# A two-layer encoder kernel on one core: early sums at the stage beginnings, and the latents' norm taken in the RWKV projections

## The chip, the cores and the metric

The kernel runs on one core of a Trainium2 chip. Its engines are TensorE (PE: matmuls; PEld: its weight loads), VectorE (DVE), ScalarE (ACT), GpSimd (POOL) and SyncE (SP), which issues all transfers here. They run side by side and meet at semaphores. The metric is the device time of one launch in microseconds; lower is better.

## What is computed

Sixteen meta tokens and 512 tokens, 1024 channels wide, pass through two layers. Cut to what matters here:

```
h = concat(meta, x)                                   # 528 x 1024
for l in range(2):
    h = h + 0.5 * rms(swiglu(rms(h, g0)), g1)
    u = rms(h, g2)
    p_rw, p_ml, p_dsa, p_gate = split(u @ w_in[l])
    y_rw, y_ml, y_dsa = rwkv7(p_rw), mlstm(p_ml), dsa(p_dsa)
    proj = branches @ w_branch[l]
    mixed = sum(sigmoid(p_gate) * proj) @ w_out[l]
    h = h + rms(mixed, g3)
    h = h + 0.5 * rms(swiglu(rms(h, g4)), g5)
# in dsa: q, c_kv, q_idx, k_idx, w_idx = split(p)
#   c_kv = rms(c_kv, kv_norm);  q_lat[h] = (q[h] @ w_uk[h]) / 8        # 8 heads of 64, latent 128
#   an index score picks 128 of the allowed positions; attention of q_lat on c_kv;
#   y = (prob @ c_kv) @ w_uv
```

## The kernel before, in words

Activations lie channels by tokens: `h` is eight tiles of 128 channels by 528 tokens, and 528 tokens are two PSUM banks of 264. The kernel is a row of stages, each a block of per-engine programs closed by a barrier: start; then in each layer FFN, RWKV (projections, recurrence, output), DSA, mLSTM, merge, FFN; at the end a post-norm and the store.

**Exact products.** A float32 product is three products of a faster type: each operand is split into a high part (ScalarE copy) and a low part (a subtraction, on GpSimd for weights in FFN, RWKV and merge, on VectorE in DSA). `exact` issues high times high, high times low, low times high. Weights come as units of four 128x128 blocks, 256 KB, through a ring; `S("split")` or `S("d_split")` counts units whose low part is made. Float32 matmuls that are not split run as two passes each, and the profile counts passes.

**A stage beginning (class `Lead`, from L315).** The stage before leaves its output in `fo` and the squares of its output channels in `ssq`: seven of eight tiles summed in `ssq[:, 2]` by `Out.add`, the last in `ssq[:, 1]`. `tensor_post` sums both over the channels on TensorE (L367; a matmul with the squares as weights and 64 columns of ones for each of five token groups), VectorE and ScalarE make the root (L409 to L412, L335), and TensorE spreads it over the channels (L374). Then for each k of eight VectorE multiplies `fo` (L429), adds to `h` (L430), and makes `u_low` (L424) from ScalarE's `u_high` (L347); ScalarE also makes the squares of `h` (L350), which TensorE sums (L400). TensorE multiplies k's block for two output tiles at once (`leading_pair`, or the loop in `phase_ffn`), 12 matmuls, as soon as `u_low` is there. The factor of this second norm is applied to the outputs. `occupy` is 128x128 matmuls on ones whose result nobody reads (L384; L831 in merge); seven such stand at the end of FFN and merge, after `out_put` has reached 5, four and twelve in a beginning.

ScalarE's order in a beginning: root, then the first two weight splits (L634, L1631), then `u_high` and squares by k, with the third split behind k=0 and the fourth behind k=1.

**RWKV projections.** 14 tiles of RWKV columns, then ten of DSA's go through one `Dense` ring of four units. GpSimd sets `s3` (L969) before its first low part. VectorE scales each tile by the row factor (L996).

**DSA beginning (`phase_dsa`, from L1695).** SyncE loads `wuk` and `wuv`, then the dense weights. ScalarE squares the latents `ckv` (L1904), TensorE sums them over channels (L1813), VectorE takes mean and reciprocal (L1973, L1974), ScalarE the root, VectorE scales (L1976). TensorE waits for all three loads, then makes `q_lat` of eight heads (L1822, 64 rows each) in two PSUM pairs in turn, ScalarE copies them out (L1910), then come eight blocks of dense work, the values (L1830), which VectorE copies out (L1984), and the first index products (L1764). ScalarE makes three weight splits behind the fourth head.

Of the kernel before, what the change touches and what calls it, by code (L numbers as in the profile page):

```python
# [13 lines left out]
ds = bass.ds  # L14
# [37 lines left out]
EARLY = 4  # L52

# [46 lines left out]
def build_program(nc, x, meta_tokens, norm_gain, ffn_w_in, ffn_w_out, w_in, rw_mu, rw_w0, rw_w_up,  # L100
# [4 lines left out]
    with ctx:  # L105
# [53 lines left out]

        def clear():  # L160
# [24 lines left out]
        def token_spread(lhs, m):  # L185
# [3 lines left out]
            return last  # L189

# [48 lines left out]
        def phase_start(st):  # L239
            xt = sb(st, "xt", [P, 5, D_MODEL])  # L240
            firstp = Params(st)
            with nc.Block() as block:
# [8 lines left out]
                def _(g):  # L251
# [5 lines left out]
                    g.memset(ones[:], 1.0)  # L257
# [30 lines left out]
                def _(pe):  # L288
# [12 lines left out]
                    firstp.turn(pe, PS[:, 2])  # L301

# [12 lines left out]
        class Lead:  # L315
# [6 lines left out]
            def __init__(self, st, ring, pre, banks, later):  # L322
# [3 lines left out]
                self.sums = PS[:, banks[0]]  # L326
# [37 lines left out]
            def column_sums(self, src, first, last):  # L364

                for j, (t0, n) in enumerate(ST_):
                    ins = nc.tensor.matmul(self.sums[0:n, 64 * j:64 * j + 64], src[:, t0:t0 + n], ones[:, 0:64],  # L367
                                           start=first and j == 0, stop=last, skip_group_check=True)
                return ins

# [22 lines left out]
            def tensor_square(self, pe, k):  # L393
                pe.wait_ge(S("squares"), k + 1)
                if not self.later:
                    self.column_sums(self.ring[k % 2], k == 0, k == KD - 1).then_inc(S("h_summed"), 1)
                    self.occupy(pe, 1 if k < KD - 1 else 4)
                    return
# [5 lines left out]
            def factor(self, v, own, x):  # L404
# [4 lines left out]
                nc.vector.tensor_scalar(rq[:, 0:full], self.sums[:, 0:64 * full:64], 1.0 / D_MODEL, EPS, ALU.mult, ALU.add)  # L409
                own(nc.vector.tensor_scalar(rq[0:m, full:full + 1], self.sums[0:m, 64 * full:64 * full + 1], 1.0 / D_MODEL,  # L410
# [3 lines left out]
            def vector(self, v):  # L414
# [101 lines left out]
        def phase_ffn(hh, hl, l, which, pre, gain, cut):  # L516

            with ExitStack() as st:
# [15 lines left out]
                with nc.Block() as block:  # L534
# [36 lines left out]
                    def _(pe):  # L571
# [18 lines left out]
                        for k in range(KD):  # L590
                            pe.wait_ge(S("u_low"), k + 1)
                            for s in range(2):
                                n = 2 * (k // 4) + s
                                if k % 4 == 0:
                                    pe.wait_ge(S("split"), n + 1 + R)
                                product(s, n, k % 4, k)
# [27 lines left out]
                        else:  # L624
                            pe.wait_ge(S("out_put"), KD - 3)
# [1917 lines left out]
```

## Time and profile before

| | |
|---|---|
| median of 3 runs | 3551.43 us (3547.36 to 3555.32) |
| profiled execution | 3546.51 us, span 3544.8 us |
| mean granted TensorE clock | 0.978 |
| TensorE busy | 3390.9 us, 96% of the span |
| VectorE, ScalarE, GpSimd busy | 1554.5, 1185.2, 1260.0 us |
| stages of layer 0 start at | FFN 15.7, RWKV 422.7, its recurrence 614.0, its output 802.7, DSA 827.4, mLSTM 1071.2, merge 1181.7, FFN 1372.4 us |
| of layer 1 | 1777.7, 2183.4, 2376.2, 2566.0, 2592.3, 2836.0, 2945.7, 3128.9 us; post-norm 3517.6 |

An operation's row gives start, duration, engine, line, what it writes and reads, the number of like operations in a row, and in brackets how long its engine had idled and what ended that. The granted clock is a share of full speed; 1.00 is 2.4 GHz and 0.50 is 1.2 GHz. A row of a stretch gives its bounds, its length, the busy time and number of instructions of PE, PEld, DVE, ACT and POOL, the granted clock, the DMA engines' busy share and GB/s.

### The profile page before, as it was taken

How to read it: one execution, taken by the hardware profiler on the slowest of the kernel's cores; microseconds unless marked ns; L12 is line 12 of the kernel's file. 1: busy time of each engine (PE TensorE's matmuls, PEld its weight loads, DVE VectorE, ACT ScalarE, POOL GpSimd, SP SyncE). 2: the span in 40 equal slices, each digit the busy share in tenths (PEclk: the TensorE clock that was granted, in tenths of full speed). 3: DMA queues.
4: the chain of work that ended last, by engine and by line, in shares of the span. 5: the costliest groups of instructions: out<-in, count | busy, mean ns of one | idle time of the engine just before them, and what ended most of it. 6: DMA issues, size and time to landing. Idle time of an engine off the chain costs nothing. (4 is left out here: it accounts for less than half of the span.)

```text
span 3544.8 us, 74221 instructions
## 1 busy us (share of the span) xinstructions
PE 3390.9 (96%) x30010; PEld 3068.4 (87%) x30010; DVE 1554.5 (44%) x2696; ACT 1185.2 (33%) x2257; POOL 1260.0 (36%) x936
## 2 busy tenths in 40 slices
PE   8999999998999999999999999999989999999998
PEld 8999999776778899999999999987767777878886
DVE  5331245445767434332053313454457684343312
ACT  3222342222455324222232223412235453342222
POOL 4444335320003443444434443343200024535542
PEclk9999999998999999999999999999989999999999
DMA  3333222001112232333223332210011122323332
GB/s 97 89 91 90 81 63 57 3 3 45 48 34 60 64 92 67 93 91 90 77 84 89 91 91 77 66 45 3 3 51 46 31 60 75 95 72 95 95 91 73
DMA packets 464410, 236.55 MB, mean 67 GB/s; under 512 B 20862, under 2 KB 462476, under 8 KB 464156
## 3 DMA queue, kind: packets, MB, share of 16 engines
q1 hardware_dynamic: 464156, 232.92, 23.5%
q8 instruction: 189, 3.10, 0.4%
q14 instruction: 65, 0.53, 0.0%
HBM read 230.50 MB, written 2.10 MB: 66 GB/s over the span
## 5 line engine op out<-in xcount | busy, mean ns | idle before, releaser
L561 POOL TENSOR_TENSOR W_low<-W,W_high 128x512 fp32r<-128x512 f32 (+1 forms) x544 | 720.8, 1326 | 877.7 <-ACT W_high L634 876.9
L156 PE MATMUL PS<-u_high,W_high 128*128 128x264 f32 (+1 forms) x2944 | 903.9, 307 | 15.6 <-DVE u_low L424 7.2
L157 PE MATMUL PS<-u_low,W_high 128*128 128x264 f32 (+1 forms) x2944 | 891.8, 303 | 0.0
L158 PE MATMUL PS<-u_high,W_low 128*128 128x264 f32 (+1 forms) x2944 | 891.6, 303 | 0.0
L634 ACT ACTIVATE W_high<-W 128x512 fp32r<-128x512 f32 (+1 forms) x544 | 335.5, 619 | 991.6 <-PE PS L158 954.7
L156 PEld LDWEIGHTS PS<-u_high,W_high 128*128 128x128 f32 x2944 | 554.5, 188 | 47.6 <-DVE u_low L424 9.6
L157 PEld LDWEIGHTS PS<-u_low,W_high 128*128 128x128 f32 x2944 | 555.0, 189 | 22.7
L158 PEld LDWEIGHTS PS<-u_high,W_low 128*128 128x128 f32 x2944 | 552.9, 188 | 22.5
L156 PE MATMUL PS<-u_high,dW_high 128*128 128x264 f32 (+1 forms) x1408 | 429.7, 305 | 15.6 <-POOL dW_low L1636 4.6
L158 PE MATMUL PS<-u_high,dW_low 128*128 128x264 f32 (+1 forms) x1408 | 405.0, 288 | 0.0
L157 PE MATMUL PS<-u_low,dW_high 128*128 128x264 f32 (+1 forms) x1408 | 404.8, 287 | 0.0
L157 PE MATMUL PS<-hidden_low,W_high 128*128 128x264 f32 (+1 forms) x1232 | 369.9, 300 | 0.0
L158 PE MATMUL PS<-hidden_high,W_low 128*128 128x264 f32 (+1 forms) x1232 | 368.9, 299 | 0.0
L156 PE MATMUL PS<-hidden_high,W_high 128*128 128x264 f32 (+1 forms) x1232 | 368.3, 299 | 0.0
L156 PEld LDWEIGHTS PS<-u_high,dW_high 128*128 128x128 f32 (+1 forms) x1408 | 270.1, 192 | 34.3 <-issue 15.6
L157 PEld LDWEIGHTS PS<-u_low,dW_high 128*128 128x128 f32 (+1 forms) x1408 | 270.4, 192 | 2.3
L158 PEld LDWEIGHTS PS<-u_high,dW_low 128*128 128x128 f32 (+1 forms) x1408 | 269.0, 191 | 0.0
L679 DVE TENSOR_TENSOR hid<-PS,rs 128x528 f32<-128x528 f32 (+1 forms) x88 | 61.9, 703 | 405.7 <-PE PS L158 404.5
L756 POOL TENSOR_TENSOR W_low<-W,W_high 128x512 fp32r<-128x512 f32 x120 | 168.6, 1405 | 197.9 <-ACT W_high L764 197.9
L156 PEld LDWEIGHTS PS<-hidden_high,W_high 128*128 128x128 f32 x1232 | 232.1, 188 | 7.4
L158 PEld LDWEIGHTS PS<-hidden_high,W_low 128*128 128x128 f32 x1232 | 231.8, 188 | 7.6
L157 PEld LDWEIGHTS PS<-hidden_low,W_high 128*128 128x128 f32 x1232 | 231.2, 188 | 7.9
(383 smaller groups left out, 5485.3 us busy)
## 6 DMA issues: line engine op xcount, KB each, us to landing
W<-in_ffn_w_in SPq DMA_DIRECT2D x352, 256.0 KB, 2.9
dW<-in_w_in SPq DMA_DIRECT2D x172, 256.0 KB, 2.9
W<-in_ffn_w_out SPq DMA_DIRECT2D x160, 256.0 KB, 2.8
W<-in_w_in SPq DMA_DIRECT2D x80, 256.0 KB, 3.0
W<-in_w_branch SPq DMA_DIRECT2D x48, 256.0 KB, 2.9
W<-in_w_out SPq DMA_DIRECT2D x32, 256.0 KB, 2.9
W<-in_ffn_w_out SPq DMA_DIRECT2D x32, 128.0 KB, 2.1
xt<-in_x SPq DMA_DIRECT2D x4, 512.0 KB, 4.6
```

The costliest lines, as they stand in the source:

```text
L156: nc.tensor.matmul(dst, wh, xh, start=first, stop=False)
L157: nc.tensor.matmul(dst, wh, xl, start=False, stop=False)
L158: return nc.tensor.matmul(dst, wl, xh, start=False, stop=final)
L561: g.tensor_tensor(WL[:, r, 0:nk], W[:, r, 0:nk], WH[:, r, 0:nk].bitcast(F32), ALU.subtract).then_inc(S("split"), 1)
L634: nc.scalar.activation(WH[:, r, 0:nk], W[:, r, 0:nk], ACT.Copy).then_inc(S("high"), 1)
L679: nc.vector.tensor_tensor(cut.of(hid[:, j]), ps(1), cut.of(rs[:]), ALU.mult).then_inc(dve_evac, 1)
L756: g.tensor_tensor(WL[:, u % R], W[:, u % R], WH[:, u % R].bitcast(F32), ALU.subtract).then_inc(S("split"), 1)
```

## The change

What it does:
1. The sums over `ssq[:, 2]` move to the end of the stage before (`early_sums`, into bank 4), with five fillers behind them instead of seven; in the start stage they run on zeros.
2. The first two output tiles take the two products with `u_high` for each k first, then the one with `u_low`. VectorE makes `u_low` of k-1 before it adds k. In FFN all of the first four weight splits stand ahead of `u_high` on ScalarE. In RWKV the setting of `s3` moves behind the eighth low part.
3. The latents' square, sum, root and scaling move into the RWKV projections, around block 168 of 192. `wuk` takes the buffer of `lora` and loads in RWKV's output part.
4. In DSA the heads start at once, in three PSUM pairs, each followed by three 128x128 fillers. Two weight splits are made during the heads, one behind the fourth and one behind the sixth, the others behind the eight dense blocks. SyncE issues two dense units ahead of `wuv`.

```diff
+        def token_square_sums(bank, src, first, last):
+            for j, (t0, n) in enumerate(ST_):
+                ins = nc.tensor.matmul(PS[0:n, bank, 64 * j:64 * j + 64], src[:, t0:t0 + n], ones[:, 0:64],
+                                       start=first and j == 0, stop=last, skip_group_check=True)
+            return ins
+        def early_sums(pe):
+            pe.wait_ge(S("out_put"), KD - 1)
+            pe.wait_ge(S("added"), KD - 2)
+            token_square_sums(POST_BANK, ssq[:, 2], True, False)
...
             def tensor_post(self, pe):
-                self.column_sums(ssq[:, 2], True, False)
-                self.column_sums(ssq[:, 1], False, True).then_inc(S("summed"), 1)
+                token_square_sums(POST_BANK, ssq[:, 1], False, True).then_inc(S("summed"), 1)
                 self.occupy(pe, 4)
...
                 for k in range(KD):
                     own(nc.vector.tensor_tensor(fo[:, k], fo[:, k], self.spread, ALU.mult))
-                    nc.vector.tensor_tensor(h[:, k], h[:, k], fo[:, k], ALU.add).then_inc(S("h_new"), 1)
                     if self.later and k:
                         low(k - 1)
+                    nc.vector.tensor_tensor(h[:, k], h[:, k], fo[:, k], ALU.add).then_inc(S("h_new"), 1)
...
                         for k in range(KD):
+                            pe.wait_ge(S("u_high"), k + 1)
+                            j, tiles = k % 4, [(s, a, cut.span(a)) for s in range(2) for a in range(cut.a)]
+                            for s, a, half in tiles:
+                                n = 2 * (k // 4) + s
+                                if j == 0 and a == 0:
+                                    pe.wait_ge(S("split"), n + 1 + R)
+                                of_high(PS[:, 2 * s + a, 0:cut.n], WH[:, n, j], WL[:, n, j], uh[:, k, half], k == 0)
                             pe.wait_ge(S("u_low"), k + 1)
...
+                            for s, a, half in tiles:
+                                last = of_low(PS[:, 2 * s + a, 0:cut.n], WH[:, n, j], ul[:, k, half], k == KD - 1)
...
-                            pe.wait_ge(S("out_put"), KD - 3)
-                            lead.occupy(pe, 7)
+                        early_sums(pe)
+                        if not nextp:
+                            lead.occupy(pe, 5)
...
-                            for n in {None: (0, 1), 0: (2,), 1: (3,), 5: (4,), 6: (5,), 7: (6,)}.get(k, ()):
+                            for n in {None: (0, 1, 2, 3), 5: (4,), 6: (5,), 7: (6,)}.get(k, ()):
...
# RWKV projections
+                    for u in range(8):
+                        dense.low(g, u)
                     g.memset(s3[:], 1.0).then_inc(S("starts"), 1)
...
+                    dense.blocks(pe, CKV_AT - dense.given)
+                    pe.wait_ge(S("ckv_squares"), 1)
+                    pe.wait_ge(S("kappa_scaled"), 4)
+                    for a in range(2):
+                        last = nc.tensor.matmul(PS[:, a, 0:H2], ones[:], ckv_sq[:, a * H2:(a + 1) * H2],
+                                                start=True, stop=True)
+                    last.then_inc(S("ckv_sum"), 1)
...
# DSA, TensorE
-                    pe.wait_ge(S("ckv_squares"), 1)
-                    for a in range(2):
-                        last = nc.tensor.matmul(PS[:, a, 0:H2], ones[:], sq[:, a * H2:(a + 1) * H2],
-                                                start=True, stop=True)
-                    last.then_inc(S("ckv_sum"), 1)
-                    pe.wait_ge(loaded, 48)
                     for hd in range(H):
-                        b, m = 64 * (hd % 2), hd % 2 + 1
-                        if hd >= 2:
-                            pe.wait_ge(S("qlat"), hd - 1)
+                        b, m = 64 * (hd % 2), hd % 3
+                        if hd >= 3:
+                            pe.wait_ge(S("qlat"), hd - 2)
...
                         last.then_inc(S("qlat_made"), 1)
+                        for _ in range(3):
+                            nc.tensor.matmul(PS[:, 6, 0:P], ones[:], ones[:], start=True, stop=True)
                     dense.blocks(pe, START[0])
-                    pe.wait_ge(S("ckv"), 1)
+                    pe.wait_ge(loaded, 16)
...
# DSA, ScalarE
-                        if hd == 3:
-                            dense.after(act, 0)
+                        if hd in (3, 5):
+                            dense.after(act, 0, upto=hd // 2)
```

## Rows read from the trace of the kernel before

**Rows 1.** Waits of TensorE over the whole span: total, times, longest.
```profile
PE PS L156 <- DVE u_low L424: 11.2, 12, 1.5
```

**Rows 2.** Timeline around the FFN beginning of layer 1: start, duration, engine, operation.
```profile
1776.38 0.69 ACT L502 ACTIVATE fo<-PS,gs 128x528 f32<-128x528 f32 x1
1777.93 2.54 PE L367 MATMUL PS<-ones,ssq 128*128 128x64 f32 x20 [1.83 <-PEq L162]
...
1784.29 2.94 PE L384 MATMUL PS<-ones 128*128 128x128 f32 x24
1784.40 0.70 DVE L429 TENSOR_TENSOR fo<-fo,PS 128x528 f32<-128x528 f32 x1 [3.36 <-PE PS L374]
...
1785.88 0.73 ACT L347 ACTIVATE u_high<-h,prm 128x528 fp32r<-128x528 f32 x1 [3.44 <-DVE h L430]
...
1787.12 0.76 DVE L424 SCALAR_TENSOR_TENSOR u_low<-h,prm,u_high 128x528 fp32r<-128x528 f32 x1
...
1787.94 0.39 PE L156 MATMUL PS<-u_high,W_high 128*128 128x264 f32 x1 [0.70 <-DVE u_low L424]
```

**Rows 3.** Stretches from the first sum of each beginning to the block of k=7.
```profile
15.75:44.81 29.06, 27.46 (x174) 25.26 (x175) 19.91 (x28) 15.05 (x25) 7.66 (x6) 0.88 0.29 84
422.77:450.59 27.82, 25.96 (x175) 23.94 (x175) 21.78 (x30) 15.42 (x25) 10.93 (x8) 0.94 0.42 109
1372.58:1400.11 27.53, 25.94 (x175) 23.87 (x175) 19.78 (x28) 15.04 (x25) 8.21 (x6) 0.94 0.33 92
1777.93:1805.49 27.56, 25.96 (x174) 23.94 (x175) 19.90 (x28) 15.14 (x25) 7.66 (x6) 0.94 0.31 88
2183.48:2210.05 26.57, 24.42 (x174) 22.49 (x175) 22.09 (x30) 15.28 (x25) 9.81 (x8) 1.00 0.44 113
3129.04:3155.43 26.39, 23.95 (x133) 20.13 (x133) 20.55 (x28) 15.08 (x25) 7.77 (x6) 1.00 0.32 91
```

**Rows 4.** Timeline from the end of the first FFN into the RWKV projections.
```profile
420.38 1.72 PE L384 MATMUL PS<-ones 128*128 128x128 f32 x14
422.77 2.54 PE L367 MATMUL PS<-ones,ssq 128*128 128x64 f32 x20 [0.67 <-PEq L162]
422.77 1.84 DVE L978 TENSOR_SCALAR omm<-prm 128x14 f32<-128x14 f32 x1 [15.49 <-PEq L162]
...
428.05 0.63 ACT L1631 ACTIVATE dW_high<-dW 128x512 fp32r<-128x512 f32 x1 [1.93 <-DMA dW<-in_w_in]
...
462.91 1.33 POOL L1636 TENSOR_TENSOR dW_low<-dW,dW_high 128x512 fp32r<-128x512 f32 x1 [9.16 <-ACT dW_high L1631]
```

**Rows 5.** Timeline of the last FFN's beginning, GpSimd and VectorE.
```profile
3133.11 2.49 POOL L561 TENSOR_TENSOR W_low<-W,W_high 128x512 fp32r<-128x512 f32 x2 [15.48 <-ACT W_high L634]
...
3134.70 1.46 DVE L430 TENSOR_TENSOR h<-h,fo 128x528 f32<-128x528 f32 x1
```

**Rows 6.** Timeline of the DSA beginning of layer 0.
```profile
828.15 1.99 PE L1813 MATMUL PS<-lg,ones 128*128 128x264 f32 x4 [2.65 <-ACT lg L1904]
...
830.91 3.45 DVE L1974 RECIPROCAL rs<-rs 128x528 f32<-128x528 f32 x1
832.18 2.14 PE L1822 MATMUL PS<-gates,wuk 64*128 64x264 f32 x8 [2.04 <-DMA wuv<-in_dsa_w_uv]
...
838.76 1.66 ACT L1631 ACTIVATE dW_high<-dW 128x512 fp32r<-128x512 f32 x3
...
843.80 0.59 PE L156 MATMUL PS<-u_high,dW_high 128*128 128x264 f32 x1
...
850.54 4.66 PE L1830 MATMUL PS<-wuv,kv_dsa 128*16 128x512 f32 x10
...
851.68 0.68 DVE L1984 COPY vh<-PS 16x512 f32<-16x512 f32 x1 [9.34 <-PE PS L1830]
```

**Rows 7.** The stretch of the last two pairs of heads in that beginning.
```profile
838.40:843.80 5.40, 5.18 (x16) 3.45 (x16) 2.72 (x9) 3.52 (x7) 0.00 (x0) 0.50 0.47 127
```

**Rows 8.** Timeline, the last work of TensorE in RWKV's output part.
```profile
824.34 1.16 PE L1522 MATMUL PS<-pj_rw,gup 128*128 128x264 f32 x4
```

More of the change, by code:

```diff
@@ L325, in __init__ @@
                 self.idle = PS[:, banks[2], 0:P]
-                self.sums = PS[:, banks[0]]
+                self.bank = banks[0]
                 self.wide_sums = PS[:, banks[0]:banks[0] + 2, 0:H2]
@@ L362, in scalar @@
                             between(act, k)
[L364 to L369, printed above, removed]
             def spread_out(self, pe, x):
@@ L907, in phase_rwkv @@
             early = st.enter_context(ExitStack())
-            lora = sb(early, "lora", [P, BW])
+            lora = wuk[:].rearrange("p a c -> p (a c)")
             th = sb(early, "th", [P, T])
@@ L1054, in _ @@
                                                            in1=ends[:, :, m], op0=ALU.mult, op1=ALU.mult))
-                    for i in range(nrw + 4, dense.tiles):
+                    for i in range(nrw + 4, nrw + 7):
+                        scaled(i)
+                    v.wait_ge(S("ckv_sum"), 1)
+                    own(nc.vector.tensor_scalar(halves(ckv_rs), PS[:, 0:2, 0:H2], 1.0 / P, EPS, ALU.mult, ALU.add))
+                    nc.vector.reciprocal(ckv_rs, ckv_rs).then_inc(S("ckv_recip"), 1)
+                    scaled(nrw + 7)
+                    v.wait_ge(S("ckv_rsqrt"), 1)
+                    nc.vector.scalar_tensor_tensor(out=ckv, in0=ckv, scalar=prm[:, G_KVN:G_KVN + 1], in1=ckv_rs,
+                                                   op0=ALU.mult, op1=ALU.mult)
+                    for i in range(nrw + 8, dense.tiles):
                         scaled(i)
@@ L1164, in _ @@
                     lead.tensor_post(pe)
-                    dense.leading_pair(pe, S("u_low"), lead.tensor_square)
+                    dense.leading_pair(pe, lead.tensor_square)
                     dense.blocks(pe, KD)
@@ L1452, in phase_rwkv, with _ @@
                 B_PAIR, S_PAIR, G_PAIR = (1, 2, 1, 2), (3, 1, 3, 1), (0, 2, 0, 2)
+                @block.sync
+                def _(sp):
+                    for b in range(2):
+                        sp.dma_start(wuk[64 * b:64 * b + 64],
+                                     dsa_w_uk[ds(l, 1)].rearrange("o (a b) d c -> b d (o a) c", b=2)[b]
+                                     ).then_inc(loaded, 16)
+                    sp.wait_ge(loaded, 32)
                 @block.vector
@@ L1692, in after, with phase_dsa @@
                     self.split += 1
[L1695 removed]
+        def phase_dsa(pj, wuk, tok, of_ml, y_of, l, st):
             H = 8
@@ L1744, in _ @@
                 def _(sp):
-                    for b in range(2):
-                        sp.dma_start(wuk[64 * b:64 * b + 64],
-                                     dsa_w_uk[ds(l, 1)].rearrange("o (a b) d c -> b d (o a) c", b=2)[b]
-                                     ).then_inc(loaded, 16)
+                    for u in range(2):
+                        dense.load(sp, u)
                     sp.dma_start(wuv[:], dsa_w_uv[ds(l, 1)].rearrange("o h c d -> c (o h) d")).then_inc(loaded, 16)
-                    for u in range(dense.units):
+                    for u in range(2, dense.units):
                         dense.load(sp, u)
```

89 lines of the change are left out of this document (51 added, 38 removed).

## The prediction

> **What bounds the kernel now.** I read the waits of TensorE first, then the timeline around each place that the diff touches, then the table of stretches. The page has TensorE busy for 96% of the span, so time is won only where it idles, where it runs at the lower of its two clock levels, or where work is taken from it. The largest wait of the projection products is for u_low, 11.2 us in 12 waits: the stage beginnings [rows 1]. A beginning is this chain [rows 2]: 20 passes of column sums, fillers, ten passes that spread the factor, then on VectorE a multiply and an add, on ScalarE u_high, again on VectorE multiply, add and u_low, and only then the first product at 1787.94. From the first sum to the product block of the last k the six beginnings take 26.4 to 29.1 us each [rows 3].
>
> The DSA beginning is the second place [rows 6]. TensorE stands from 825.5 to 828.15, makes the latents' sum, stands for 2.04 us for wuv, makes the qlat products of eight heads in pairs that run side by side (eight passes in 2.14 us; one head uses rows 0 to 63, the next 64 to 127) and reaches the first dense block only at 843.80, 16.4 us after the stage starts at 827.45. All this runs at half clock: 0.50 in the stretch where TensorE is 96% busy [rows 7].
>
> **Sums moved to the end of the stage before.** At a start, 10 of 20 passes go; 20 take 2.54 us, so 1.27 us. At the end of the stage before, 14 filler passes (1.72 us) become 10 sum passes and 10 filler passes, 1.27 + 1.23 = 2.5 us. TensorE's end is what releases the next stage (last pass near 422.1, next stage 422.77 [rows 4]), so each stage starts 0.8 us later. Two exceptions: behind the second FFN of layer 0 ScalarE's last copy ends at 1777.07 [rows 2] and covers part of it, 0.4 us later; behind the start stage GpSimd's masks cover it all, 0.
>
> **First block on u_high, u_low later.** u_high of k=0 is there at 1785.88 + 0.73 = 1786.61, u_low at 1787.88 [rows 2]: 1.27 us earlier. From the block of k=0 to that of k=7 pass 17.55 us (1787.94 to 1805.49, the end in rows 3); at the pitch of 12 products of 0.12 us and 4 sum passes of 0.22 us, 2.35 us, seven take 16.5. So up to 1.05 us of waiting goes too. Together 1.27 + 1.27 + 1.05 = 3.6 us at most.
>
> What eats into it: VectorE now makes u_low of k-1 ahead of the add of k, and so has to sit out ScalarE's u_high (0.73 us, covered by a multiply of 0.70 but for some 0.2). Its period becomes about 2.2 us, just under the pitch. And in FFN stages all four weight splits go ahead of u_high: GpSimd is busy 4 x 1.25 us, until about 2.6 us behind the first multiply. In the start at 3129.04 the add that met such a split took 1.46 us instead of 0.71 [rows 5]. I take two such holds, 1.4 us in all; bounds are 0 (all splits end in the shadow of the spread) and 3.6 (nothing is left). So an FFN beginning of 27.5 us becomes 25.4. The start at 3129.04 ran at full clock and takes 26.39 already: it gets 1.0. In the first FFN (29.06 us, clock 0.88) I put 26.3.
>
> In RWKV the splits are bound by the weights' arrival: ScalarE waits for them until 428.05, 5.3 us behind the start [rows 4], and u_high stands behind two of them in its queue. These transfers start with the stage and so move with it. I put 25.9 us for 27.82 and 26.57. Moving the memset behind the eighth split frees a small operation of VectorE, which took 1.84 us against it, but the passes on TensorE cover that; in its new place it lies in the 9.16 us that GpSimd idles before its ninth split [rows 4]. Nothing for it; were the gap not there, 2 us a layer.
>
> Sum, each with its later start: first FFN -2.75; RWKV layer 0 27.82 - 25.9 - 0.8 = -1.1; FFN 27.53 - 25.4 - 0.8 = -1.35; FFN layer 1 27.56 - 25.4 - 0.4 = -1.8; RWKV layer 1 +0.1; last FFN 26.39 - 25.4 - 0.8 = -0.2; last post-norm -0.25. **Beginnings: -7.35 us.**
>
> **Latents' norm in the RWKV projections.** Four passes like those of the gates, 1.16 us with their tail [rows 8], cost TensorE 0.9 us a layer. ScalarE's square and VectorE's 0.71 + 3.45 us [rows 6] fall where the dense tiles come 5.8 us apart, and both are idle most of that; the tiles' PSUM banks are freed before they are wanted. **+1.8 us** in all; if the reciprocal held a tile back, at most its 3.45 us a layer more.
>
> **DSA.** Gone are the latents' four passes (1.99 us), the wait for wuv and the waits for ScalarE. Their work is no longer on the path, but each head is now followed by three fillers (six passes). These are full-row passes, so the heads no longer run side by side: at full clock 4 x 0.22 + 6 x 0.12 + 0.2 for the two changes of shape = 1.8 us a head, 14.6 us for eight. The first dense block comes 1.8 us earlier than before. The eight blocks behind it, 6.74 us at clock 0.88 [rows 6], take 48 x 0.12 = 5.8 at full: 0.95. Against this: ScalarE makes two splits during the heads instead of three [rows 6], the third only behind the eight blocks, and VectorE waits for it ahead of wi and the value copies. The first copy comes at +0.61 (tile out) +0.6 (split) +0.65 (low part) +1.0 (wi) instead of +1.1 us, and the index products wait for the fourth: they come 5.8 instead of 4.6 us behind the blocks, +1.3. **-1.45 us a layer, -2.9.** Bounds: heads with no cost for changes of shape, -3.1 a layer; the low clock, below.
>
> The weights' order (wuv behind two units) and wuk's load in RWKV's output part (802.7 to 826.8, no other transfer) cost nothing.
>
> Against this stands how the clock behaved: it fell right behind 827.4, with TensorE idle for 2.65 us; now it idles for 2.0 (825.5 to 827.5). And it did not come back while TensorE was 96% busy with 64-row products [rows 7], only after dense blocks had begun. The Trainium skill (TensorE: Matmul & The Clock Gate, What's actually happening) says that the clock follows how busy TensorE has recently been; by that alone eight heads and their fillers back to back would run at full clock, and the DSA term stands. The trace disagrees with it in that row. I take full clock as somewhat likelier, because fillers of this shape were followed by full clock in the starts (24 passes of them in 2.94 us [rows 2]).
>
> **The sum:** -7.35 + 1.8 - 2.9 = -8.45 us. The profiled execution has 3546.5 us (span 3544.8), the median is 3551.4; I take the difference off the median: **3543.0 us**.
>
> **Rivals.**
> 1. *Low clock in DSA* (slower). If the clock falls at the DSA start and 64-row heads hold it down, a head costs 4 x 0.44 + 6 x 0.23 + 0.4 = 3.5 us; eight are 28, less 0.9 for what runs before it falls. The first dense block then comes 10.5 us later than before, with the copies +11.8 a layer, so 3551.4 - 7.35 + 1.8 + 23.6 = 3569.5. For it: the row at 0.50. Against: the fillers use all rows and the idle time is shorter. It decides from a head of over 2.2 us on. In one layer alone: 3556.
> 2. *The beginnings give nothing back.* VectorE, held by four splits, becomes the bound of all eight k; only the early sums less the later start remain, -2 in all, and with DSA -3: 3548 to 3551. For it: VectorE's period is within 0.15 us of the pitch.
> 3. *All of it holds.* No holds by GpSimd, no cost between shapes: -9.5 - 6.2 + 1.8 = 3537.5.
>
> **Chances.** Forecast (3539 to 3547) 0.44; rival 1 in both layers 0.18, in one 0.10; rival 2 0.16; rival 3 0.12. Range: 3533 to 3560, from rival 3 with some margin to rival 1 in one layer; only both layers at low clock lie outside. The bound of what can be told from no change is 0.2%, 7.1 us, so 3544.3 is where faster begins: from the forecast 0.32, rival 3 0.12, rival 2 0.02, in all 0.46 faster; the same 0.12 + 0.12 + 0.06 = 0.30; slower 0.24.
>
> **What would show it.** Right: the first product of a beginning waits for u_high and comes about 7.5 us behind the sums' start; block of k=7 at 25 to 26 us; the sum of four passes inside RWKV with no wait around it; DSA's first dense block 14 to 15 us behind the stage start with the clock at 1.00, and VectorE's copies late by 1.3. Wrong: a granted clock of 0.50 over the qlat products; adds over 1.4 us at every k; waits for u_high at k=3 to 7.

## The result and the profile after

The changed kernel takes 3564.56 us (median of 6 runs, 3559.7 to 3569.42) against 3551.28 us of the kernel before in the same runs (3545.72 to 3555.32): ratio 1.0041, 95% interval 1.0029 to 1.0052. It is 13.3 us slower. The forecast was 3543.0; the first rival, low clock in DSA in both layers, gave 3569.5.

The stages in the two traces, from barrier to barrier, in us:

| stage | before | after | difference |
|---|---|---|---|
| first FFN, layer 0 | 407.2 | 404.4 | -2.8 |
| RWKV projections, layer 0 | 191.2 | 191.3 | 0.0 |
| RWKV recurrence and output, layer 0 | 213.5 | 215.8 | +2.3 |
| **DSA, layer 0** | 243.8 | 257.9 | **+14.1** |
| mLSTM and merge, layer 0 | 301.2 | 301.6 | +0.4 |
| second FFN, layer 0 | 405.4 | 405.3 | -0.1 |
| first FFN, layer 1 | 405.7 | 406.3 | +0.6 |
| RWKV projections, layer 1 | 192.7 | 187.6 | -5.1 |
| RWKV recurrence and output, layer 1 | 216.1 | 215.9 | -0.2 |
| **DSA, layer 1** | 243.7 | 258.0 | **+14.2** |
| mLSTM and merge, layer 1 | 292.8 | 291.2 | -1.6 |
| second FFN, layer 1 | 388.9 | 389.5 | +0.6 |
| post-norm | 16.4 | 15.6 | -0.8 |

All the loss, and more, is in the two DSA stages: 28.3 us. The rest, the short start and end stages included, sums to -6.4 us. These are the windows of the DSA beginning of layer 0, from the first head to the first dense block, and over the eight blocks (bounds, length, busy time and count of PE, PEld, DVE, ACT, POOL, granted clock, DMA share, GB/s):

```profile
826.98:855.39 28.41, 28.41 (x80) 19.81 (x81) 1.38 (x2) 5.92 (x10) 0.00 (x0) 0.51 0.21 55
855.39:862.61 7.22, 7.22 (x51) 7.08 (x50) 0.00 (x0) 0.00 (x0) 0.00 (x0) 0.81 0.01 2
```

TensorE is never idle in the first row, and its clock is at the lower level, 1.2 GHz (0.51 is 0.50 with a short piece of full clock at the start). The timeline of the same place shows one head and its fillers, at 3.6 us a head (826.98 to 830.24 partly at full clock, then 830.24 to 833.87):

```profile
826.98 1.74 PE L1880 MATMUL PS<-gates,lora_or_wuk 64*128 64x264 f32 x4 [1.98 <-PEq L171]
...
828.65 1.65 PE L1885 MATMUL PS<-ones 128*128 128x128 f32 x6
...
830.24 2.13 PE L1880 MATMUL PS<-gates,lora_or_wuk 64*128 64x264 f32 x4
```

This answers to [rows 6, 7]. There two heads stood next to each other and took eight passes in 2.14 us; here one head alone takes four passes in 2.13 us. The wait for `wuv` and the latents' sum are gone from the path, as meant; the first dense block nevertheless comes 28.4 us behind the stage start instead of 16.4.

The six stage beginnings, from the first sum to the block of k=7, answer to [rows 3]:

```profile
15.74:41.22 25.48, 25.48 (x165) 23.97 (x165) 16.91 (x28) 15.21 (x25) 8.31 (x6) 0.88 0.33 92
419.96:444.15 24.19, 23.22 (x165) 21.58 (x165) 18.29 (x30) 15.16 (x25) 9.90 (x6) 1.00 0.45 121
1386.62:1413.82 27.20, 24.89 (x164) 22.96 (x165) 17.98 (x28) 15.14 (x25) 8.37 (x6) 0.94 0.33 91
1791.90:1819.30 27.40, 24.99 (x164) 22.94 (x165) 18.48 (x28) 15.05 (x25) 8.87 (x6) 0.94 0.31 86
2198.09:2220.99 22.90, 22.82 (x164) 21.44 (x165) 17.02 (x30) 15.18 (x25) 9.22 (x6) 1.00 0.48 126
3150.91:3175.82 24.91, 23.04 (x122) 18.89 (x123) 18.18 (x28) 14.65 (x25) 8.47 (x6) 1.00 0.32 90
```

The RWKV beginnings won 3.6 and 3.7 us, more than forecast. The two FFN beginnings in the middle won 0.3 and 0.2 us, where 2.1 were forecast. The timeline of the second FFN of layer 0 shows what holds them (the bracket tells how long the engine had idled, and what ended it):

```profile
1389.73 0.63 ACT L660 ACTIVATE W_high<-W 128x512 fp32r<-128x512 f32 x1 [0.92 <-DMA W<-in_ffn_w_in]
...
1390.54 5.62 POOL L580 TENSOR_TENSOR W_low<-W,W_high 128x512 fp32r<-128x512 f32 x4 [16.89 <-ACT W_high L660]
...
1391.11 1.26 DVE L451 TENSOR_TENSOR h<-h,fo 128x528 f32<-128x528 f32 x1
...
1394.06 0.63 ACT L660 ACTIVATE W_high<-W 128x512 fp32r<-128x512 f32 x1 [1.58 <-DMA W<-in_ffn_w_in]
1394.60 0.72 ACT L373 ACTIVATE u_high<-h,prm 128x528 fp32r<-128x528 f32 x1
...
1395.37 0.39 PE L163 MATMUL PS<-u_high,W_high 128*128 128x264 f32 x1 [2.16 <-ACT u_high L373]
```

`h` of k=0 is there at 1392.37, but ScalarE stands for 1.58 us at the fourth weight split, whose unit has not landed, and `u_high` is behind it in ScalarE's queue. TensorE waits 2.16 us for `u_high`. Shortly behind it, from 1397.4 to 1400.8, the granted clock is 0.50, and 1.00 before and after. In the first FFN of layer 1 all four splits come late, the first only 5.5 us behind the stage start after a wait of 3.00 us for its unit, and TensorE waits 0.99 us for a low part.

### The profile page after: what moved, and what is told of

Same layout as the page of the kernel before. It is cut to its first block and busy times, and to the rows that moved or that the text cites. A ratio compares the mean times of both kernels' runs of the same rounds, so it can differ in the third digit from the quotient of the medians.

```text
span 3566.7 us, 74424 instructions
## 1 busy us (share of the span) xinstructions
PE 3422.0 (96%) x30086; PEld 3093.1 (87%) x30086; DVE 1549.3 (43%) x2696; ACT 1186.0 (33%) x2257; POOL 1265.2 (35%) x936
## 5 line engine op out<-in xcount | busy, mean ns | idle before, releaser
L157 PE MATMUL PS<-u_high,W_high 128*128 128x264 f32 (+1 forms) x2832 | 865.8, 306 | 8.4 <-DVEq L459 3.4
L159 PE MATMUL PS<-u_high,W_low 128*128 128x264 f32 (+1 forms) x2832 | 859.8, 304 | 0.0
L158 PE MATMUL PS<-u_low,W_high 128*128 128x264 f32 (+1 forms) x2832 | 859.2, 303 | 0.0
L157 PEld LDWEIGHTS PS<-u_high,W_high 128*128 128x128 f32 x2832 | 534.1, 189 | 36.7 <-issue 6.3
L158 PEld LDWEIGHTS PS<-u_low,W_high 128*128 128x128 f32 x2832 | 535.2, 189 | 21.8
L159 PEld LDWEIGHTS PS<-u_high,W_low 128*128 128x128 f32 x2832 | 532.2, 188 | 21.5
L157 PE MATMUL PS<-u_high,dW_high 128*128 128x264 f32 (+1 forms) x1344 | 410.8, 306 | 11.8 <-POOL dW_low L1696 5.0
L159 PE MATMUL PS<-u_high,dW_low 128*128 128x264 f32 (+1 forms) x1344 | 388.2, 289 | 0.0
L158 PE MATMUL PS<-u_low,dW_high 128*128 128x264 f32 (+1 forms) x1344 | 388.1, 289 | 0.0
L532 DVE TENSOR_TENSOR ssq<-ssq 128x528 f32<-128x528 f32 (+1 forms) x36 | 51.4, 1427 | 430.9 <-ACT ssq L520 422.1
```

Source lines behind the costliest of these rows:

```text
L157: nc.tensor.matmul(dst, wh, xh, start=first, stop=False)
L158: nc.tensor.matmul(dst, wh, xl, start=False, stop=False)
L159: return nc.tensor.matmul(dst, wl, xh, start=False, stop=final)
L532: nc.vector.tensor_tensor(ssq[:, 2, t], ssq[:, 2, t] if m > 1 else ssq[:, 0, t], ssq[:, m % 2, t], ALU.add).then_inc(S("added"), 1)
```

## The experiments

Unless said otherwise, a time is the median of the runs, and the kernel before ran on the same chip in between: 3549.99 us for `starts_only`, `dsa_only`, `heads_bare` and `heads_full_rows`; 3551.02 for `pairs_6fill`, `heads_8fill`, `ffn_splits` and `heads_around`; 3548.54 for `two_pairs`, `third_split`, `held_clock` and `all_three`.

### The two halves of the change

`starts_only` is the kernel before with parts 1 and 2 of the change, `dsa_only` the kernel before with parts 3 and 4. Every line of either stands in the kernel before or in the changed one.

> The kernel before with the stage beginnings of the change alone (parts 1 and 2); DSA and the latents' norm as before. If the low clock over the qlat heads is what made the changed kernel slower, the DSA stages are back at 243.7 us each and the rest keeps its gain: the two profiled kernels differ by +21.9 us, of which the DSA stages have +28.3, so the rest is -6.4; without the latents' sum in RWKV (1.8) it is about -8: 3543, between 3540 and 3547. If the new beginnings give nothing back, as my second rival has it: 3549 to 3551.

Measured: 3538.06 us, ratio 0.9964 (0.995 to 0.9978). The DSA stages take 243.8 and 244.6 us. The new beginnings give back more than I thought (3540 to 3547), some 12 us by the medians and 7.8 by the two traces' spans (3544.8 to 3537.0; the traced execution of the kernel before, 3546.51 us, is 3.5 under its median here). The rival that they give nothing is out.

> The kernel before with the latents' norm and the DSA beginning of the change alone (parts 3 and 4). Low clock over the heads caused by the heads themselves: DSA stages of 257 to 258 us each, granted clock 0.50 over them, first dense block 28 us behind the stage start, in all +28.3 + 1.8: 3581. If the low clock came from the way the new stage beginnings shift the work, DSA here runs its heads at 1.00 and the kernel takes 3550 or less.

Measured: 3576.47 us, ratio 1.0072 (1.0056 to 1.0089). The DSA stages take 257.3 us each, 13.5 more than before. So the loss comes with the DSA part whatever stands around it. The time is 4.5 us under the 3581 expected; the 1.8 us that I had charged for the latents' norm do not show in the RWKV projections, which take 192.1 and 191.8 us against 191.2 and 192.7 before. The halves sum to -11.9 + 26.5 = +14.6 us, and the whole change measured +13.3.

### What holds the clock down

`heads_bare` leaves out the fillers and nothing else:

```diff
                         last.then_inc(S("qlat_made"), 1)
-                        for _ in range(3):
-                            nc.tensor.matmul(PS[:, 6, 0:P], ones[:], ones[:], start=True, stop=True)
```

> The changed kernel without the three filler products behind each head of DSA; nothing of the computation is left out. The clock stays at 0.50 over the heads, but two heads run side by side again: four pairs of 2.14 us, first dense block at 8.5 to 9.5 us behind the stage start instead of 28.4, the eight blocks behind it up to 3 us longer at the low clock. Some 18 us less a layer: 3528, between 3522 and 3534. Rival: ScalarE's copies and weight splits become the bound and the low clock lasts through the eight blocks, first dense block at 12, blocks 11 us: 3540.

Measured: 3517.27 us, ratio 0.9906 (0.9889 to 0.9922): 33 us faster than the kernel before, and, each set against the kernel before in its own runs, 46 faster than the changed kernel. The rival (3540) is out. My own figure (3522 to 3534) was too high as well, since the clock comes back within the heads. Its windows over the eight heads and over the eight blocks:

```profile
826.28:833.33 7.05, 7.05 (x33) 5.54 (x33) 0.78 (x2) 4.49 (x9) 0.00 (x0) 0.76 0.58 149
833.33:839.33 6.00, 6.00 (x49) 5.86 (x48) 0.61 (x1) 0.88 (x2) 0.00 (x0) 1.00 0.34 87
```

Eight heads take 7.05 us in place of 28.4, and the blocks behind them run at full clock.

`heads_full_rows` keeps the fillers and lets the head's products use all 128 rows. It leaves the computation: two heads are summed, so the attention's logits are others.

```diff
-last = nc.tensor.matmul(PS[:, 2 * m + a, 0:H2], wuk[b:b + 64, hd // 2],
-                        pj[Q0 + hd // 2][b:b + 64, a * H2:(a + 1) * H2],
+last = nc.tensor.matmul(PS[:, 2 * m + a, 0:H2], wuk[:, hd // 2],
+                        pj[Q0 + hd // 2][:, a * H2:(a + 1) * H2],
```

> The changed kernel with the qlat products reading all 128 rows of wuk and of q (two heads summed, so the attention's logits are not those of the reference); count, columns and fillers as in the changed kernel. If it is the half-filled rows that hold the clock down, it rises to 1.00 during the heads and the first dense block comes 15 to 20 us behind the stage start instead of 28.4: about 3543. If rows do not matter (idle time at the start, or the small passes, decide), the clock stays at 0.50 to the end of the heads and the first dense block stays at 28: 3564.

Measured: one run, 3533.68 us, with the first dense block 14.1 us behind the first head in both layers, a little less than the 15 to 20 expected. The rows from its timeline and its windows:

```profile
829.23 1.06 PE L1880 MATMUL PS<-gates,lora_or_wuk 128*128 128x264 f32 x4
830.12 0.83 PE L1885 MATMUL PS<-ones 128*128 128x128 f32 x6
```

```profile
828.40:838.51 10.11, 10.11 (x69) 9.30 (x67) 1.38 (x2) 5.08 (x9) 0.00 (x0) 1.00 0.26 64
```

The instructions have the same number, columns and order as in the changed kernel, and the start of the stage has the same idle time (1.98 us). Only the rows differ (and with them the changes between 64-row and 128-row products, of which there are none here). From 828.40, 4.0 us behind the first head, the clock is 1.00 and stays there.

`pairs_6fill` keeps all 24 fillers and the reference's computation, but puts six behind every second head:

```diff
-                        for _ in range(3):
+                        for _ in range(6 * (hd % 2)):
```

> The changed kernel with the same 24 fillers, but six behind every second head, so that the two heads of a pair stand next to each other and can run side by side on rows 0 to 63 and 64 to 127. If the fillers did harm by parting the pairs, the pair fills all rows again, the clock rises to 1.00 within the first pairs and the first dense block comes 11 to 15 us behind the stage start instead of 28.4. If fillers of 128 columns hold the clock down wherever they stand, the pairs take 2.1 + 3.3 us each at 0.50, first dense block at 22.

Measured: one run, 3535.87 us, first dense block at 12.0 us in both layers. Timeline and window:

```profile
831.32 1.17 PE L1880 MATMUL PS<-gates,lora_or_wuk 64*128 64x264 f32 x8
...
832.42 1.60 PE L1885 MATMUL PS<-ones 128*128 128x128 f32 x12
```

```profile
827.08:831.32 4.24, 4.24 (x21) 3.45 (x21) 0.00 (x0) 1.11 (x2) 0.00 (x0) 0.60 0.76 194
831.32:839.28 7.96, 7.96 (x63) 6.55 (x63) 1.39 (x2) 4.37 (x8) 0.00 (x0) 1.00 0.30 75
```

This is the cleanest of the comparisons: the same instructions as in the changed kernel in another order, 16.4 us earlier at the first dense block. A pair is eight passes in 1.17 us at full clock. A head alone takes 1.16 us for its four (`heads_8fill`, below), so the second head of a pair costs almost nothing.

`heads_8fill` goes the other way, eight fillers behind each head instead of three.

> The changed kernel with eight fillers behind each head instead of three. If it is the mean filling of TensorE's rows that decides the clock, heads now are 4 passes of half the rows to 16 of all of them, and the clock rises to 1.00 during the heads: 2.8 to 3.1 us a head, first dense block 24 to 27 us behind the stage start. If 64-row products by themselves hold the clock down, it stays at 0.50: 2.1 + 4.4 = 6.4 us a head, first dense block at 51.

Measured: one run, 3560.22 us, first dense block 29.1 us (layer 0) and 25.9 us (layer 1) behind the first head; I had expected 24 to 27. Windows of both layers, and a head with its fillers at full clock:

```profile
827.06:837.70 10.64, 10.58 (x39) 8.68 (x40) 0.00 (x0) 1.22 (x2) 0.00 (x0) 0.52 0.38 99
837.70:856.25 18.55, 18.55 (x123) 15.33 (x123) 1.39 (x2) 4.70 (x8) 0.00 (x0) 1.00 0.11 29
2598.34:2602.40 4.06, 4.01 (x16) 3.29 (x17) 0.00 (x0) 0.61 (x1) 0.00 (x0) 0.59 0.70 169
```

```profile
841.10 1.16 PE L1880 MATMUL PS<-gates,lora_or_wuk 64*128 64x264 f32 x4
842.18 2.05 PE L1885 MATMUL PS<-ones 128*128 128x128 f32 x16
844.16 1.15 PE L1880 MATMUL PS<-gates,lora_or_wuk 64*128 64x264 f32 x4
```

More work between the same heads lets the clock rise, after 10.6 us in one layer and 4.1 in the other. So a 64-row product does not by itself hold the clock down; how much of the time it takes matters. As a remedy it buys nothing: it spends on fillers what the clock gives.

`two_pairs` is `heads_bare` with two PSUM pairs in turn, as before the change, instead of three:

```diff
-                        b, m = 64 * (hd % 2), hd % 3
-                        if hd >= 3:
-                            pe.wait_ge(S("qlat"), hd - 2)
+                        b, m = 64 * (hd % 2), hd % 2 + 1
+                        if hd >= 2:
+                            pe.wait_ge(S("qlat"), hd - 1)
...
# ScalarE
-                        m = hd % 3
+                        m = hd % 2 + 1
```

> The kernel without fillers between the heads, but the heads in two PSUM pairs in turn, as in the kernel before, instead of three. If it is the third PSUM pair that lets two heads stay side by side without waiting for ScalarE, the pairs take 2.8 us each again as before (starts of pairs at 835.6, 838.4, 841.2), the rows are filled half of the time and the clock stays at 0.50 over the heads: first dense block at 11 to 12 us behind the stage start instead of 7.1, eight blocks 1 us longer, 10 to 12 us slower in all: 3528. If the early start and the lack of fillers were enough for the clock to come back, it stays at 3517 to 3520.

Measured: 3529.39 us, ratio 0.9947 (0.9931 to 0.9964), first dense block at 10.3 us. A row of its timeline, and the window:

```profile
830.94 2.63 PE L1880 MATMUL PS<-gates,lora_or_wuk 64*128 64x264 f32 x8 [0.20 <-ACT qlat L1965]
```

```profile
826.02:836.37 10.35, 9.34 (x33) 5.97 (x33) 1.38 (x2) 4.81 (x9) 0.00 (x0) 0.54 0.49 127
```

With two pairs each head waits for ScalarE's copy of the head two before it, the second of a pair starts late (2.63 us for eight passes), and the clock stays down to the end of the heads. That is what [rows 7] showed: 96% busy, at 0.50. So with no fillers the third PSUM pair is worth some 12 us. No run has the change's fillers with two pairs; with heads 3.6 us apart and a copy of 0.61 us there is little that a third pair could give there.

One thing goes along with the half-filled rows in the changed kernel: the changes between 64-row and 128-row products, which seem to cost time of their own. At full clock a head is followed by its first filler after 1.08 us in `heads_8fill` and after 0.89 in `heads_full_rows` (829.23 to 830.12), with the same four passes. `heads_full_rows` has no such changes and `pairs_6fill` half as many, so these two runs alone do not part them from the rows. `two_pairs` and the kernel before have none among their heads and stay at half clock, so the changes are not needed for it. Whether they add to the low clock in the changed kernel is not shown.

### The FFN beginnings

`ffn_splits` is `heads_bare` with two of ScalarE's splits moved:

```diff
-for n in {None: (0, 1, 2, 3), 5: (4,), 6: (5,), 7: (6,)}.get(k, ()):
+for n in {None: (0, 1), 1: (2,), 2: (3,), 5: (4,), 6: (5,), 7: (6,)}.get(k, ()):
```

> The kernel without fillers between the heads, and in FFN the third and fourth weight splits of ScalarE behind the second and third u_high instead of ahead of the first. If u_high stood behind weights that land late (in the changed kernel TensorE waited 2.16 us for it in the second FFN of layer 0), the first product comes at 6.7 us behind the stage start instead of 7.5 to 8.9, whatever the transfers do, and the four FFN stages are 0.8 to 1.5 us shorter each but the first: 3514 against 3517. If GpSimd's holds of VectorE are what counts, they only move to later k and the block of k=7 stays where it is: 3517.

Measured: 3512.4 us, ratio 0.9895 (0.9879 to 0.9912), the fastest kernel of the study. Against `heads_bare` that is 4.9 us by the medians and 5.7 by the spans (3515.6 and 3509.9). The intervals of the two ratios overlap, so the time alone does not part them; the stages do. The four FFN stages take 403.2, 401.3, 401.9 and 386.1 us against 404.3, 403.7, 404.3 and 388.5, which is 8.3 us less, and part of it is lost again in other stages. The place shown above for the changed kernel, and the window of that beginning:

```profile
1366.18 0.74 ACT L373 ACTIVATE u_high<-h,prm 128x528 fp32r<-128x528 f32 x1 [1.18 <-DVE h L451]
...
1366.96 0.39 PE L163 MATMUL PS<-u_high,W_high 128*128 128x264 f32 x1
```

```profile
1360.42:1383.60 23.18, 23.18 (x164) 21.41 (x165) 16.92 (x28) 14.73 (x25) 8.94 (x6) 1.00 0.36 102
```

`u_high` now waits for `h` and for nothing else, the first product comes 6.54 us behind the first sum (8.75 in the changed kernel), and TensorE does not stand once in 23 us, nor in the beginnings at 1761.67 and 3097.61. Of GpSimd's holds of VectorE the one at the first add remains (1.24 us).

The edit does two things, though. It takes the splits from ahead of `u_high`, and with them it moves GpSimd's third and fourth low part away from VectorE's add of k=1. `heads_bare`, in which the splits land in time, shows both in the same beginning:

```profile
1369.56 0.39 PE L163 MATMUL PS<-u_high,W_high 128*128 128x264 f32 x1 [0.89 <-ACT u_high L373]
...
1370.75 1.78 DVE L451 TENSOR_TENSOR h<-h,fo 128x528 f32<-128x528 f32 x1
...
1373.36 0.39 PE L163 MATMUL PS<-u_high,W_high 128*128 128x264 f32 x1 [0.82 <-ACT u_high L373]
```

The first wait is the queue's: `u_high` starts behind the fourth split, 0.9 us after `h` is ready. The second is for `u_high` of k=1, whose add took 1.78 us where it takes 0.70 in `ffn_splits`. So the order in ScalarE's queue is shown for the first wait, in the changed kernel above all (2.16 us); how the gain of a stage divides between the two is not shown.

### Four attempts to win more in the DSA beginning

`heads_around` is `heads_bare` with the eight dense blocks between the fourth and the fifth head, and ScalarE's first four splits among the first four copies.

```diff
                     for hd in range(H):
+                        if hd == 4:
+                            dense.blocks(pe, START[0])
...
-                    dense.blocks(pe, START[0])
...
-                        if hd in (3, 5):
-                            dense.after(act, 0, upto=hd // 2)
-                    dense.after(act, START[0])
+                        if hd in (1, 2):
+                            dense.after(act, 0, upto=hd)
+                        if hd == 3:
+                            dense.after(act, 0)
+                            dense.after(act, START[0])
```

> The kernel without fillers between the heads; four heads, then the eight dense blocks, then the other four heads, and ScalarE makes all four first splits during the first four heads. The dense blocks start as soon as their weights are split, 5.5 to 6 us behind the stage start, and fill the rows early; the value products start at 13.5 instead of 13.1 us if nothing is won, at 11.5 if the heads' second half runs side by side at full clock; the value copies no longer wait for a split (0.9 less). 3517 - 2 x 2 = 3513, between 3510 and 3517. Rival: the weights land too late (their split is ready at 5.5 us or later, with TensorE idle before), and the kernel stays at 3517.

Measured: 3525.19 us, ratio 0.9924 (0.9908 to 0.9941): 8 us slower than `heads_bare` by the medians, where I expected 4 faster. TensorE's rows and one of ScalarE's in layer 0, and a window over the four heads and the first blocks:

```profile
826.54 4.30 PE L1882 MATMUL PS<-gates,lora_or_wuk 64*128 64x264 f32 x16 [1.98 <-PEq L171]
...
838.24 2.04 PE L1882 MATMUL PS<-gates,lora_or_wuk 64*128 64x264 f32 x12
838.85 1.14 ACT L1691 ACTIVATE dW_high<-dW 128x512 fp32r<-128x512 f32 x2
...
840.54 1.15 PE L1882 MATMUL PS<-gates,lora_or_wuk 64*128 64x264 f32 x4 [0.26 <-ACT qlat L1966]
...
842.49 1.02 PE L1889 MATMUL PS<-wuv,kv_dsa 128*16 128x512 f32 x2 [0.79 <-ACT qlat L1966]
```

```profile
826.54:834.00 7.46, 7.46 (x30) 6.23 (x31) 1.77 (x3) 4.00 (x7) 0.00 (x0) 0.54 0.69 179
```

The weights were in time. But the blocks now run where the clock is low, and the last heads wait behind a tile's copy and two splits of ScalarE; the values start at 15.95 us instead of 13.05, and in layer 1 at 18.31 instead of 12.98. The low stretch should be spent on work that is cheap in it, and the heads are that.

`third_split` is `ffn_splits` with ScalarE's third split behind the eighth head. `held_clock` is `ffn_splits` with five fillers at the end of RWKV's output part. `all_three` has the fillers, the first two splits behind the second and fourth head, and the next two behind the eighth.

```diff
# third_split
-                        if hd in (3, 5):
+                        if hd in (3, 5, 7):
                             dense.after(act, 0, upto=hd // 2)
# held_clock
                         gates(m)
+                    pe.wait_ge(S("scaled"), 4)
+                    for _ in range(5):
+                        nc.tensor.matmul(PS[:, 6, 0:P], ones[:], ones[:], start=True, stop=True)
# all_three: held_clock, and
-                        if hd in (3, 5):
-                            dense.after(act, 0, upto=hd // 2)
+                        if hd in (1, 3, 7):
+                            dense.after(act, 0, upto=(hd + 1) // 2)
```

> The kernel with the FFN splits behind u_high and no fillers between the heads, plus ScalarE's third split behind the eighth head instead of behind the eight dense blocks. By my working, VectorE's value copies then no longer wait for it and the index products come up to 0.9 us earlier a layer (TensorE waits 0.89 us for the copy): 3510.8 against 3512.4. If the copies are bound by the value products themselves (one in 0.93 us), 3512.4 stays.

> The kernel with the FFN splits behind u_high and no fillers between the heads, plus five fillers at the end of RWKV's output part, in the 1.27 us in which VectorE finishes. TensorE is then idle for 0.7 us ahead of DSA instead of 1.98. If the idle time lets the clock fall, it now holds at 1.00 into the heads, which end at 3.6 to 4.5 instead of 7.1 us; the dense blocks then wait for ScalarE's splits and start at 6 us: 1 us a layer, 3510 against 3512.4. If the heads themselves lower it, nothing changes: 3512.

> Both additions together, and ScalarE's first two splits behind the second and fourth head instead of the fourth and sixth. The splits are then no bound for the dense blocks, which start 5 to 5.5 us behind the stage start instead of 7.1, if the weights are there (they were split at 2.9 us in the kernel with dense blocks between the heads): 2 us a layer, and 0.9 for the copies: 3507 against 3512.4, between 3504 and 3511. Rival: a split that stands ahead of a head's copy holds the heads up as it did there, and nothing is won: 3512 or more.

Measured: 3512.9, 3513.24 and 3513.81 us; ratios 0.9902 (0.9886 to 0.9919), 0.9902 (0.9885 to 0.9918), 0.9906 (0.989 to 0.9923). None is told apart from `ffn_splits` (0.9895). Yet at the place itself two of them do what they should. In `third_split` the ninth dense block, the first behind the index products, starts 18.09 instead of 19.04 us behind the first head. In `held_clock` the clock is 1.00 from the first head on, and the first dense block comes at 5.8 (layer 0, first row below) and 6.35 us (layer 1) instead of 7.04. What was won is given back some 20 us later. The second row is of `held_clock`:

```profile
826.78:832.63 5.85, 5.85 (x33) 4.50 (x33) 0.84 (x2) 4.44 (x9) 0.00 (x0) 1.00 0.71 179
854.50:861.30 6.80, 6.12 (x27) 5.62 (x27) 4.58 (x24) 2.06 (x7) 0.00 (x0) 0.50 0.15 39
```

The next row is of `third_split`, and the one below it is the same stretch of `ffn_splits`:

```profile
853.20:860.00 6.80, 6.08 (x27) 5.62 (x27) 4.62 (x24) 2.10 (x7) 0.00 (x0) 0.50 0.15 39
```

```profile
853.20:860.00 6.80, 5.47 (x43) 4.84 (x41) 5.16 (x27) 3.61 (x11) 0.00 (x0) 1.00 0.10 26
```

A low stretch of 6.8 us has appeared in the lightly loaded part behind, where `ffn_splits` has full clock (it has one of 3.4 us over its heads, which `held_clock` lacks). Why it appears there when the work before it moves by a microsecond I did not settle.

`all_three` met its rival. ScalarE's first split stands ahead of the third copy and waits for its weights, 0.69 us in layer 0 and 1.55 in layer 1, and TensorE waits for the copy behind it:

```profile
828.96 2.67 PE L1883 MATMUL PS<-gates,lora_or_wuk 64*128 64x264 f32 x12 [0.67 <-ACT qlat L1968]
...
2574.16 2.79 PE L1883 MATMUL PS<-gates,lora_or_wuk 64*128 64x264 f32 x12 [1.52 <-ACT qlat L1968]
```

Its first dense block comes at 6.75 and 7.7 us where I had expected 5 to 5.5.

## Why the prediction was wrong, step by step

**Which step failed.** "I take full clock as somewhat likelier, because fillers of this shape were followed by full clock in the starts." In both layers the granted clock was 0.51 over the eight heads, 0.50 but for a short piece at the start. What happened is the first rival, nearly in its numbers: 3.6 us a head where it said 3.5, first dense block 12.1 us later than before where it said 10.5, the time 3564.6 where it said 3569.5. It had a chance of 0.18 for both layers, and the stated range left it out.

**Why it failed.** Both halves of the reason stood in the prediction and were not put together. It said that full-row fillers keep the heads from running side by side, and priced that as time at full clock. It said that 64-row products had stood at 0.50 while TensorE was 96% busy, and left that as an odd row. Parted by fillers, each head fills half of the rows for 2.1 of 3.6 us. The runs vary this one at a time. The same instructions on all rows: clock 1.00 (`heads_full_rows`). The same fillers with the pairs left together: 1.00 (`pairs_6fill`). More full-row work between single heads: 1.00, late (`heads_8fill`). No fillers, but heads that start apart by a wait: 0.54 (`two_pairs`). No fillers and no wait: 0.76 over the heads, 1.00 behind them (`heads_bare`). The cited rule of the Trainium skill (TensorE: Matmul & The Clock Gate, What's actually happening), that the clock follows how busy TensorE has been, fits these runs only if busy is read as how much of the array is filled, and not as the busy share of the profile: the changed kernel was 100% busy at 0.51. That 64-row tiles on different rows can run in parallel stands in the Trainium skill (TensorEngine Tiling (Array Packing), Key Properties); the traces agree, with eight passes of a pair in 1.17 us where four of one head take 1.16.

**Heads at full clock.** Forecast 1.8 us a head, 0.2 of it for the two changes of shape, for which the prediction names no row. `heads_8fill` has such heads at full clock: 3.06 us for a head and 16 filler passes (841.10 to 844.16), less ten passes of 0.12, is 1.86. The size was right had the clock held. With full rows and no change of shape, four passes take 0.89 us and six fillers 0.67 (`heads_full_rows`, 829.23 to 830.79), so by that pitch 3.06 would be 2.68: the 64 rows and the two changes of shape cost some 0.4 us, not 0.2. The forecast's 14.6 us for eight should be 14.4 by its own 1.8.

**Eight blocks.** Forecast 5.8 us at full clock, measured 7.22 at 0.81; `heads_bare` has them at 1.00, in 6.00.

**The stage beginnings.** Forecast -7.35 us. `starts_only` gave 7.8 by the spans and 12 by the medians. That the spans agree with the forecast is luck: 5.1 us of theirs come from the RWKV projections of layer 1 (187.6 for 192.7 us), where the forecast had nothing, and the total hides two errors of opposite sign. RWKV: 25.9 us forecast, 24.2 and 22.9 measured; the splits that I took as bound by the weights' arrival did not hold `u_high` up (it waits for `h` from k=1 on). FFN: 25.4 forecast; 27.2, 27.4 and 24.9 measured. I charged GpSimd's holds of VectorE (1.4 us), and they are in the trace (the add at 1391.11 takes 1.26 us, not 0.71). But they are longer than that where they fall on the add of k=1 (1.78 us in `heads_bare`). And one item I had not seen: `u_high` behind the fourth weight split, which waits for a transfer. `ffn_splits` takes both away, and with them 2.4 us in each FFN stage but the first, 1.1 there.

**The later start.** Forecast 0.8 us a stage. From the first filler or early sum to the next stage's first sum: 422.77 - 420.38 = 2.39 before [rows 4], 419.96 - 416.76 = 3.20 after; 0.81. Right.

**The latents' norm in RWKV.** Forecast 0.9 us a layer on TensorE and no wait. The timeline of the changed kernel:

```profile
588.42 1.05 PE L1235 MATMUL PS<-wide,ones 128*128 128x264 f32 x4
...
589.51 0.71 DVE L1089 TENSOR_SCALAR wide<-PS 128x528 f32<-128x528 f32 x1 [0.18 <-PE PS L1235]
```

TensorE does not wait before or behind it. Right as to the waits. The load of `wuk` shows no cost either: RWKV's output part takes 26.3 and 26.2 us, and 26.4 and 26.5 in `starts_only`, which does not have it there.

**VectorE's copies.** Forecast: index products 5.8 us behind the blocks instead of 4.6. Measured:

```profile
862.61 4.66 PE L1890 MATMUL PS<-wuv,kv_dsa 128*16 128x512 f32 x10
...
865.64 3.07 DVE L2035 COPY vh<-PS 16x512 f32<-16x512 f32 x5
...
868.16 0.52 PE L1828 MATMUL PS<-kv_dsa,gates 64*128 64x144 f32 x4 [0.89 <-DVE vh L2035]
```

868.16 - 862.61 = 5.55 us. Right in kind; the forecast had 0.25 too much.

**What no term had.** The RWKV projections of layer 0 won 3.6 us in their beginning and nothing as a stage; those of layer 1 won 3.7 and 5.1. In layer 0 the changed kernel has stretches at 0.50 of 3.4 and 10.2 us behind the beginning, where the kernel before has one of 6.8:

```profile
458.70:462.10 3.40, 3.40 (x18) 3.40 (x17) 2.56 (x3) 2.39 (x5) 2.78 (x4) 0.50 0.33 82
499.70:509.90 10.20, 10.20 (x51) 10.11 (x51) 0.55 (x1) 0.00 (x0) 1.68 (x1) 0.50 0.15 42
```

At half clock 6.8 us more cost some 3.4, about what is missing. In layer 1 it is the other way round, with 3.4 and 10.2 us before (2224.3 to 2227.7 and 2265.3 to 2275.5) and 6.8 after (2277.9 to 2284.7): the 5.1 us won there are in good part this. Such stretches come and go with the time at which a stage begins, in kernels that share that stage's code, and make 2 to 4 us of scatter between stages that I can neither forecast nor read as a gain.

## What to carry to other kernels

TensorE's busy share did not say whether its clock would hold: look at the granted clock beside the number of rows that the products fill. Products on 64 rows belong next to each other in pairs on the two halves, with enough PSUM buffers that neither waits; here a filler between them parted the pair and cost twice, once for the lost overlap and again for the clock. And what stands first in an in-order queue should not wait for a transfer when something behind it is on the path: two weight splits moved behind `u_high` took 8.3 us from the FFN stages, some of it by keeping GpSimd off VectorE's adds, and some 5 from the whole.

## What the runs showed of the hardware that I had not expected

- TensorE can be 100% busy for 28.4 us and stay at 1.2 GHz (0.51), when 64-row products take 2.1 of every 3.6 us. With all 128 rows in the same instructions it was at 2.4 GHz from 4.0 us behind the first head on.
- Two 64-row heads of four passes each take 1.17 us side by side at full clock, one alone takes 1.16, and four passes with 128 rows take 1.06.
- At full clock it takes 1.08 us from the start of a 64-row head to its first full-row filler (`heads_8fill`), and 0.89 when the head uses all rows (`heads_full_rows`), with the same four passes.
- Moving work by about 1 us made a stretch of 6.8 us at 0.50 appear some 20 us later (`held_clock`, `third_split`), which took the gain back.
